# A two-layer transformer forward pass in one launch: the feed-forward remainders' buffer moved by 64 bytes

## What is computed

```
h = rmsnorm(x, attn_pre_norm); proj = h @ w_in          # 1024 -> attention inputs
x = x + rmsnorm(mixed @ w_out, attn_post_norm)
h = rmsnorm(x, ffn_pre_norm)
u = causal_depthwise_conv(h @ w_up, conv_w, conv_b)     # 1024 -> 5632
x = x + rmsnorm((gelu(gate) * up) @ w_down, ffn_post_norm)   # 2816 -> 1024
# two layers of the second kind:
x = x + gate_m * (attention(h @ w_qkv) @ w_o   or   retention(h @ w_in) @ w_o)
x = x + gate_f * ((silu(g) * up) @ w_down)              # h @ w_gate_up, 1024 -> 5632
```

## Time and profile before

| | |
|---|---|
| time, median of 3 runs | 1045.28 us (1044.31 to 1046.72) |
| the profiled execution's own time | 1042.57 us |
| its span, first to last instruction | 1040.8 us |
| PE busy | 1024.4 us (98%), 7860 matmuls |
| PE's weight loads busy | 974.9 us (94%) |
| DVE, ACT, POOL busy | 77%, 57%, 16% |
| PE in the chain that ended last | 87% |
| HBM | 219 GB/s over the span |

### The profile page before, as it was taken

How to read it: one execution, slowest core, us unless ns; L and a number is a source line. 1 busy time by engine, 2 the same in 40 slices (tenths; PEclk the granted TensorE clock), 3 DMA queues, 4 the chain that set the end, 5 groups by cost and what they waited for, 6 DMA issues and landing times.

```text
span 1040.8 us, 19237 instructions
## 1 busy us (share of the span) xinstructions
PE 1024.4 (98%) x7860; PEld 974.9 (94%) x7860; DVE 804.5 (77%) x1378; ACT 592.5 (57%) x1027; POOL 165.4 (16%) x172
## 2 busy tenths in 40 slices
PE   8999999999999999999999999999999999999997
PEld 7988898999889997999999999988999999999997
DVE  5877799999997977588999788885678576674443
ACT  5688676666446766665444455443465566544443
POOL 1000134333102100032212011201100123111010
PEclk8999999999999999999999999999999999999999
DMA  9733356776894433457998787653435546774441
GB/s 364 266 117 123 122 195 243 282 285 248 342 401 146 157 126 118 188 191 275 377 370 308 288 322 271 202 196 127 163 122 186 179 142 235 280 260 148 168 168 41
DMA packets 34132, 227.49 MB, mean 219 GB/s; under 512 B 3795, under 2 KB 4092, under 8 KB 10492
## 3 DMA queue, kind: packets, MB, share of 16 engines
q1 hardware_dynamic: 33596, 223.63, 58.9%
q0 software_dynamic: 448, 2.63, 0.6%
HBM read 225.19 MB, written 2.63 MB: 219 GB/s over the span
## 4 chain that ended last, share of the span: by engine, by line
PE 87%; DVE 9%; ACT 2%; issue 1%; DMA 1%; POOL 0%; SPq 0%; POOLq 0%; ACTq 0%; DVEq 0%
PE psum L1506 21%; PE psum L1508 21%; PE psum L1507 21%; DVE w_lo L2258 3%; PE psum L1571 2%; PE psum L1574 2%; PE psum L1573 2%; PE psum L1922 2%; PE psum L1924 2%; PE psum L1923 2%; PE psum L1713 1%; ACT w_hi L820 1%; DVE arena L2582 1%; PE psum L1868 1%; PE psum L1605 1%
## 5 line engine op out<-in xcount | busy, mean ns | idle before, releaser
L2258 DVE TENSOR_TENSOR w_lo<-raw,w_hi 128x1024 fp32r<-128x1024 f32 (+2 forms) x340 | 387.3, 1160 | 143.5 <-ACT w_hi L820 137.8
L820 ACT ACTIVATE w_hi<-raw 128x1024 fp32r<-128x1024 f32 (+2 forms) x340 | 333.4, 996 | 210.3 <-PE psum L1508 155.7
L1506 PE MATMUL psum<-h_hi,w_hi 128*128 128x256 f32 (+1 forms) x1144 | 324.3, 283 | 5.1 <-DVE w_lo L2258 2.6
L1508 PE MATMUL psum<-h_hi,w_lo 128*128 128x256 f32 (+1 forms) x1144 | 320.1, 280 | 0.0
L1507 PE MATMUL psum<-h_lo,w_hi 128*128 128x256 f32 (+1 forms) x1144 | 319.9, 280 | 0.0
L1506 PE MATMUL psum<-hid_hi,w_hi 128*128 128x256 f32 (+1 forms) x952 | 270.9, 285 | 0.5 <-DVE w_lo L2258 0.4
L1507 PE MATMUL psum<-hid_lo,w_hi 128*128 128x256 f32 (+1 forms) x952 | 268.1, 282 | 0.0
L1508 PE MATMUL psum<-hid_hi,w_lo 128*128 128x256 f32 (+1 forms) x952 | 268.1, 282 | 0.0
L1506 PEld LDWEIGHTS psum<-h_hi,w_hi 128*128 128x128 f32 x1144 | 214.8, 188 | 8.5 <-DVE w_lo L2258 5.1
L1507 PEld LDWEIGHTS psum<-h_lo,w_hi 128*128 128x128 f32 x1144 | 215.7, 189 | 0.7 <-issue 0.7
L1508 PEld LDWEIGHTS psum<-h_hi,w_lo 128*128 128x128 f32 x1144 | 215.2, 188 | 0.0
(11 more groups left out here) (297 smaller groups left out, 1221.2 us busy)
## 6 DMA issues: line engine op xcount, KB each, us to landing
arena<-in_ada SPq DMA_DIRECT2D x48, 1024.0 KB, 6.6
raw<-in_gu SPq DMA_DIRECT2D x44, 1024.0 KB, 6.7
raw<-in_ret_in SPq DMA_DIRECT2D x24, 1024.0 KB, 4.9
raw<-in_up SPq DMA_DIRECT2D x22, 1024.0 KB, 4.9
raw<-in_dn SPq DMA_DIRECT2D x32, 704.0 KB, 4.2
raw<-in_qkv SPq DMA_DIRECT2D x12, 1024.0 KB, 5.0
raw<-in_down SPq DMA_DIRECT2D x11, 1024.0 KB, 7.9
raw<-in_ret_o SPq DMA_DIRECT2D x8, 1024.0 KB, 4.9
```

The lines of the kernel that those rows point to most:

```text
L820: nc.scalar.activation(w_hi[chunk % SPLIT_SLOTS][:, a:b], raw[chunk % RAW_SLOTS][:, a:b], ACT.Copy)\
L1506: nc.tensor.matmul(out, w[0], hc, start=start, stop=False, skip_group_check=True)
L1508: return nc.tensor.matmul(out, w[1], hc, start=False, stop=stop, skip_group_check=True)
L2258: tt(w_lo[s][:, a:b], raw[chunk % RAW_SLOTS][:, a:b], w_hi[s][:, a:b].bitcast(F32), ALU.subtract)\
```

## The change

A tensor `between` of 16 float32 columns (64 bytes) that nothing reads or writes is put between `hid_hi` and `hid_lo`:

```diff
         h_hi, h_lo = sb("h_hi", DT * ZW, F32R), sb("h_lo", DT * ZW, F32R)
-        hid_hi, hid_lo = sb("hid_hi", FT * S, F32R), sb("hid_lo", FT * S, F32R)
+        hid_hi, between, hid_lo = sb("hid_hi", FT * S, F32R), sb("between", 16), sb("hid_lo", FT * S, F32R)
         x = sb("x", DT * S)
```

## The result

The changed kernel takes 1048.68 us in the median (22 runs), the kernel before 1044.69 us (22 runs on the same chips). The ratio is 1.0035, with a 95% interval of 1.0027 to 1.0043, so it is slower by 3.7 us, between 2.8 and 4.5. The forecast was 1044.5 us and no difference that could be told from none. The slower rival had 1048.2 us. The profiled execution took 1049.11 us, with a span of 1047.3 us.

A forecast was written before the change was run, and what follows sets the result against it. PE, busy 98% of the span, was taken to bound the kernel through matmul start-to-start distance. Terms -1.06 + 0.56 + 0.12 - 0.39 = -0.77 us took the median 1045.28 to 1044.5 us; range 1041.8 to 1048.7.

The forecast's parts named there:

- The slower rival: All streamed `hid` phases catch the slow rhythm, 2262 matmuls x 1.3 ns = +2.9 us, 1048.2 us; chance 0.20.
- That the change acts through PE's distances alone: Whole kernel: no instruction moves, so only matmul start-to-start distance, or other engines' instructions with slack nearly everywhere, can act.
- the writers: POOL and DVE write `hid_lo` 64 bytes higher: taken as 0, within ±0.1 us.
- The rival by which addresses play no part: `hid`'s 118.7 ns comes from something else in its phases; every count stays, 1045.3 us; chance 0.15.
- That the distance from hi to lo makes the rhythm: Streamed `hid` gets `h`'s rhythms, 117.7 or 120.0 ns, by taking `h`'s hi-to-lo offset of 64 bytes.
- its own sign of this: `dn0`, `dn1`, `ret_o` below 117.7 or above 120.0 ns would mean place against the weights or moved `arena` counts.
- `hid` has one rhythm: Streamed `hid` before the change: a single rhythm of 118.7 ns, where `h` has two.
- Each will go at 117.7 or 120.0 if the distance makes `h`'s rhythm: 2262 streamed `hid` matmuls of 256 columns: -1.0 ns each if quick, +1.3 ns if slow.
- `dn0` and `dn1` keep the quick rhythm as they are entered without a stop: They follow `gu0` and `gu1`: 352 blocks x 3 x -1.0 ns = -1.06 us.
- `ret_in`'s long run and `att_o` slow, +0.56 us: Starts behind a stop or between attention pieces: (81 + 63) blocks x 3 x 1.3 ns.
- `ret_o` and the other part of `ret_in` half and half, +0.12 us: 258 blocks behind short norm-matmul breaks, mixed rhythms: 0.15 ns per matmul; ends -0.77 and +1.01 us.
- The 512-column streams, -0.39 us: `hid` as loaded operand, 552 matmuls: half of a 1.4 ns gain taken; ends -0.77 and 0.

The follow-up runs named there:

- e1_rest: Kernel before with 64 unused bytes behind `hid_lo`, so `x`, constants and `arena` move and `hid_lo` does not; 1045.82 us, ratio 1.0003.
- e2_as_h: Kernel before with `mod` and `ident` laid ahead of `hid_hi` and `warm` between, giving `hid` the places of `h`; 1043.47 us, ratio 0.9984.
- e9_hid33: Kernel before with `warm` (64 bytes) laid ahead of `hid_hi`, so `hid_hi` and `hid_lo` both move by 64 bytes; 1033.49 us, ratio 0.9887.
- e4_d512: Kernel before with `ident` laid between `hid_hi` and `hid_lo`, distance 22,528 + 512 bytes, `hid_hi` unmoved; 1044.74 us, ratio 0.9998.
- e14_after_two: Changed kernel with two more matmuls on a constant tile ahead of `dn0` and of `dn1`; 1047.02 us, ratio 1.0011 to the kernel before.
- e13: Against the kernel before, `hid_hi` and `hid_lo` both three 64-byte steps from the weights, `h_hi` at 0, `h_lo` at 3; 1032.43 us, ratio 0.9876.
- e11: Against the kernel before, `h` and `hid`, hi and lo alike, all three steps of 64 bytes from the weights; 1033.81 us, ratio 0.9888.

## Why the prediction was wrong, point by point

**That the change acts through PE's distances alone held.** The other engines hardly changed; the cost of `between` was nil and that of the writers too; `x`, the constants and `arena` cost nothing that could be told from none (e1_rest, 1.0003). The rival by which addresses play no part is refuted: the same matmul starts after 113.2 to 121.2 ns, by layout.

**That the distance from hi to lo makes the rhythm did not.** The prediction named its own sign of this, a distance above 120.0 ns in `dn0`, `dn1` and `ret_o`, and 121 came. Of the two causes that it gave for that case, e1_rest rules out the moved `arena`, and e2_as_h and e9_hid33 point to the place against the weights.

**`hid` has one rhythm: wrong.** It had shown 118.7 in four stretches, but (2, 2) also has 120.0 (`dn0` in e1_rest and in e4_d512). I read "one value seen" as "one value possible".

**Each will go at 117.7 or 120.0 if the distance makes `h`'s rhythm: wrong, and the step that failed first.** The diff says "as h's", and I took over the values of `h` with the distance. The rhythms depend on both places against the weights. At (2, 3) the bad one is 121.1, at (0, 1), the same distance, it is 120.0 (e2_as_h). The prediction did name the different place of `hid_hi`, and used it only as an argument inside the slower rival; a third value beyond the two had no price.

**`dn0` and `dn1` keep the quick rhythm as they are entered without a stop: wrong, the step that decided the sign.** The term of -1.06 us came out at 528 x 2.5 + 528 x 2.3 = +2.5 us. In the changed kernel `dn1` follows quick `gu1` and `dn0` slow `gu0`, and both were at 121. A transition between buffers changes the places under the running rhythm, so what was caught before is no sure guide. That this crossing is what picks the rhythm is argued and not shown; two matmuls inserted there went with another rhythm in both (e14_after_two).

**`ret_in`'s long run and `att_o` slow, +0.56 us: wrong sign.** They were quick, about -0.4 us. `ret_in` stood behind the same kind of stop as slow `up`; the stop does not fix the rhythm either, as `up` in e1_rest shows as well.

**`ret_o` and the other part of `ret_in` half and half, +0.12 us: mis-sized.** `ret_o` alone was wholly in the slow rhythm: 531 x 2.3 = +1.2 us.

**The 512-column streams, -0.39 us: nil.** 135 matmuls in 31 us before and after.

**The slower rival** had the right mechanism and nearly the right sum for half wrong reasons: it had 1.3 ns on 2262 matmuls, and the truth was 2.4 ns on some 1590 and a small gain on others. That the sum came so near is luck. With 2.4 in place of 1.3 the slow share need only be above 0.57, not above the 0.84 that I asked of it, and it was 1590 / 2262 = 0.70; its chance should have been higher. The range held the median by a hair, 1048.68 against 1048.7, and that is luck too, as its upper end had the wrong price and the wrong share.

**Still open:** what in the chip makes the steps of 64 bytes and the modulus of 256, and by what rule a start picks among a layout's rhythms. Of the 16 pairs of places, thirteen were tried (one more at a half step), most in one or two profiles, and a rhythm not seen in one is not excluded. The modulus is at most 512 by e4_d512; that it is 256 is only supported, by e13, where `hid` stood at 448 bytes from the weights' place and had the rhythm that e9 has at 192, and by e11, where it stood at 704 and had it in `ret_o`. `e13` is within the interval of e9, so which of the two layouts is better isn't settled.

## What to carry to other kernels

Where PE is the bound and streams float32r tiles while it loads weights, measure the start-to-start distance by stretch and try a few start addresses of the streamed buffers against the weights, in steps of 64 bytes: it costs one line, and the layouts tried here took from 1.0038 to 0.9876 of the time. Move hi and lo together and watch both; here equal places at an odd step from the weights gave the lowest distance. A distance read in one profile is one of several that the layout allows, so price such a change by the best and worst value that any layout has shown, and read the profiles of several executions.

## What the runs showed of the hardware

- The distance between starts of the same matmul (128 x 128 weights, 256 float32r columns, clock granted in full at 2.4 GHz) took the values 113.4, 116.6, 117.0, 117.8, 118.7, 120.0 and 121.1 ns by layout. None was as low as 109.2 ns, an estimate for 256 columns by the Trainium skill's rule of columns / 2.4 GHz + about 2.5 ns ("TensorE: Matmul & The Clock Gate", section "Wait — 56ns, not 53.3ns?"); the measurement decides.
- A layout can have several such rhythms (117.8 and 120.0 ns for `h` at (0, 1), 118.7 and 120.0 for `hid` at (2, 2)); each lasts for hundreds of matmuls once caught, and in e11_h33_hid33 weight loads that began 40 ns late were followed by a change from 113.2 to 117.8 ns for the rest of `up`.
- `gu0` in unchanged `h` was at 117.8 in the profile of before and at 120.1 in that of the changed kernel, 1.7 us. That is of the size of the scatter between runs of one kernel (1042.5 to 1047.56 us before); that it makes all of that scatter was not tested.
